# Two fused transformer blocks on one Trainium2 core: the second attention's rotation gets its swapped quarters by transfers inside SBUF in place of products with a swap matrix

## The reference, cut to what matters

```python
def rope_half(x, ang):
    n = x.shape[-1] // 2
    x1, x2 = x[..., :n], x[..., n:]
    cos, sin = jnp.cos(ang).astype(x.dtype), jnp.sin(ang).astype(x.dtype)
    return jnp.concatenate([x1 * cos - x2 * sin, x1 * sin + x2 * cos], axis=-1)

def axial_rope(x, row_ang, col_ang):
    return jnp.concatenate([rope_half(x[..., :AXIAL_DIM], row_ang),
                            rope_half(x[..., AXIAL_DIM:], col_ang)], axis=-1)
    ...
    q = axial_rope(rmsnorm_2(q.reshape(B, S, N_Q_HEADS, HEAD_DIM), q_gain), row_ang, col_ang)
    k = axial_rope(rmsnorm_2(k.reshape(B, S, N_KV_HEADS, HEAD_DIM), k_gain), row_ang, col_ang)
```

## Time and profile before

| | us |
|---|---|
| median of 3 runs (lowest, highest) | 1326.78 (1326.47, 1327.3) |
| the profiled execution | 1326.74 |
| its span from first to last instruction | 1325.0 |
| TensorE busy | 1264.7 (95%) |
| VectorE busy | 711.0 (54%) |
| ScalarE busy | 545.7 (41%) |
| GpSimd busy | 533.5 (40%) |

### The profile page before, as it was taken

How to read it: one execution, slowest core, us unless ns; L and a number is a source line. 1 busy time by engine, 2 the same in 40 slices (tenths; PEclk the granted TensorE clock), 3 DMA queues, 4 the chain that set the end, 5 groups by cost and what they waited for, 6 DMA issues and landing times.

```text
span 1325.0 us, 20731 instructions
## 1 busy us (share of the span) xinstructions
PE 1264.7 (95%) x8300; PEld 1003.5 (76%) x8300; DVE 711.0 (54%) x827; ACT 545.7 (41%) x734; POOL 533.5 (40%) x245
## 2 busy tenths in 40 slices
PE   5999999888899999999999999999999999999995
PEld 3777757677777877788888888888776777777873
DVE  8788756757559533336224143144477755442833
ACT  5332253244253433543223122235332468885342
POOL 4443222710157742274444444445443332223453
PEclk9999999989899999999999999999999999999998
DMA  6571111110045221122223332222422322112221
GB/s 218 160 229 64 64 48 53 59 35 4 12 158 163 100 78 51 48 96 96 95 95 96 101 102 100 96 96 96 144 88 80 108 75 65 64 65 67 99 90 64
DMA packets 35098, 119.91 MB, mean 91 GB/s; under 512 B 4544, under 2 KB 4672, under 8 KB 34624
## 3 DMA queue, kind: packets, MB, share of 16 engines
q1 hardware_dynamic: 29808, 105.78, 24.0%
q10 hardware_dynamic: 5200, 12.85, 3.1%
HBM read 111.01 MB, written 2.10 MB: 85 GB/s over the span
## 4 chain that ended last, share of the span: by engine, by line
PE 78%; DVE 14%; ACT 4%; issue 2%; ACTq 1%; DMA 1%; POOL 0%; DVEq 0%; SPq 0%
PE banks L1383 20%; PE banks L1385 19%; PE banks L1384 19%; DVE y_mid L831 2%; DVE tmp L831 1%; PE banks L1846 1%; PE banks L1404 1%; PE banks L1862 1%; PE banks L1406 1%; PE banks L1405 1%; PE banks L1951 1%; DVE qk L831 1%; PE banks L1936 1%; PE banks L1611 1%; DVE yk L831 1%
## 5 line engine op out<-in xcount | busy, mean ns | idle before, releaser
L338 POOL TENSOR_TENSOR w_lo<-w_raw,w_hi 128x1024 fp32r<-128x1024 f32 x145 | 353.7, 2440 | 536.9 <-ACT w_hi L401 536.7
L401 ACT ACTIVATE w_hi<-w_raw 128x1024 fp32r<-128x1024 f32 x145 | 153.9, 1062 | 333.2 <-PE banks L1385 213.1
L1383 PE MATMUL banks<-a_hi,w_hi 128*128 128x512 f32 x584 | 235.2, 403 | 15.5 <-DVE a_lo L839 13.4
L1385 PE MATMUL banks<-a_hi,w_lo 128*128 128x512 f32 x616 | 241.1, 391 | 0.0
L1384 PE MATMUL banks<-a_lo,w_hi 128*128 128x512 f32 x584 | 228.5, 391 | 0.0
L1385 PE MATMUL banks<-b_hi,w_lo 128*128 128x512 f32 x384 | 149.5, 389 | 0.0
L1383 PEld LDWEIGHTS banks<-a_hi,w_hi 128*128 128x128 f32 x584 | 110.1, 188 | 50.2 <-issue 17.8
L1385 PEld LDWEIGHTS banks<-a_hi,w_lo 128*128 128x128 f32 x616 | 116.2, 189 | 24.9
L831 DVE TENSOR_TENSOR x_res<-banks,x_res 128x512 f32<-128x512 f32 x56 | 38.7, 692 | 178.5 <-PE banks L1385 178.3
L338 POOL TENSOR_TENSOR w_lo<-w_raw,w_hi_mlp 128x1024 fp32r<-128x1024 f32 x36 | 87.3, 2425 | 107.7 <-ACT w_hi_mlp L401 107.7
L1384 PEld LDWEIGHTS banks<-a_lo,w_hi 128*128 128x128 f32 x584 | 110.3, 189 | 21.6 <-issue 0.7
(11 more groups left out here) (372 smaller groups left out, 2389.5 us busy)
## 6 DMA issues: line engine op xcount, KB each, us to landing
w_raw<-in_weights SPq DMA_DIRECT2D x189, 512.0 KB, 3.3
x_in<-in_x SPq DMA_DIRECT2D x4, 512.0 KB, 6.7
rot<-qk ACTq DMA_DIRECT2D x32, 64.0 KB, 2.1
decay<-in_decay ACTq DMA_DIRECT2D x1, 2048.0 KB, 8.9
x_res<-in_x ACTq DMA_DIRECT2D x4, 512.0 KB, 5.5
out_fm<-x_res SPq DMA_DIRECT2D x8, 256.0 KB, 2.1
consts<-in_consts SPq DMA_DIRECT2D x1, 1209.0 KB, 12.0
q_twice<-q_twice ACTq DMA_DIRECT2D x8, 128.0 KB, 3.6
```

The costliest lines, as they stand in the source:

```text
L338: nc.gpsimd.tensor_tensor(o, a, b, op).then_inc(S(name), 1)
L401: return nc.scalar.activation(o, a, f, **kw)
L1383: mm(o, high[:, w], hi[:, kc, :], start=kc == first, stop=False)
L1385: done = mm(o, w_lo[:, s % 4, w], hi[:, kc, :], start=False, stop=kc == last)
```

## The change

The swap matrix goes out of the constants and the product with it out of qk_norm. In its place ScalarE's queue gets swap_quarters(f): eight transfers of 16 partitions x 2 KB from qk2 to a new tile rot2 (two slots), in its iterations S_U (tiles 0 and 1), S_U+2, S_U+3 and S_GA (tiles 2, 3, 4). They stand behind head_hi and head_stack of the same iteration and ahead of gelu. They wait for the gains (qg_ready) and, from tile 2 on, until tile f-2 is rotated, whose slot they use. VectorE waits for their landing and reads rot2 where it read the bank. The minus sign of the swap matrix moves into the table of sines.

```diff
+        rot2 = at("rot2", 166, [P, 2, T])
...
+            def swap_quarters(f):
+
+                act.wait_ge(S("qg_ready"), f + 1)
+                if f >= 2:
+                    act.wait_ge(S("qk2_ready"), f - 1)
+                q = HD // 4
+                for r in range(0, P, q):
+                    o = r ^ q
+                    act.dma_start(rot2[o:o + q, f % 2, :], qk2[r:r + q, f, :]).then_inc(S(f"rot_loaded{f % 2}"), 16)
...
+                for f in {S_U: (0, 1), S_U + 2: (2,), S_U + 3: (3,), S_GA: (4,)}.get(s, ()):
+                    swap_quarters(f)
                 if S_U < s <= S_GA:
                     f = s - S_U - 1
                     act.wait_ge(S("tile_taken"), S_U + f + 1)
...
             def axial_rope(f):
 
-                dve.wait_ge(S("rot_done"), f + 1)
-                step(tt(tmp2[:, 0, :], psum[2 + f % 2][:], axial[:, 1, :], ALU.mult))
+                dve.wait_ge(S(f"rot_loaded{f % 2}"), 16 * (16 + 8 * (f // 2 + 1)))
+                step(tt(tmp2[:, 0, :], rot2[:, f % 2, :], axial[:, 1, :], ALU.mult))
...
                 if f >= 2:
                     pe.wait_ge(S("qk2_ready"), f - 1)
-                mm(psum[2 + f % 2][:], C("swap_ax"), qk2[:, f, :], start=True, stop=True).then_inc(S("rot_done"), 1)
                 spread_parts(psum[4 + f % 2][:], f, rn2_hi[0:10, :], rn2_lo[0:10, :]).then_inc(S("spread2_done"), 1)
...
-    axial = np.stack([np.cos(ang), np.sin(ang)], axis=1).astype(f32)
+    sign = np.where(i % half < quart, -1.0, 1.0)[:, None]
+    axial = np.stack([np.cos(ang), sign * np.sin(ang)], axis=1).astype(f32)
```

More of the change, by code:

```diff
@@ L55 @@
 CONSTS = [("eps6", 1), ("eps64", 1), ("inv_freq", 1), ("kg_scale", 1), ("kg_eps", 1), ("kg_min", 1),
-          ("ident", 128), ("ones", 128), ("blockones", 128), ("center", 128), ("swap_ax", 128),
+          ("ident", 128), ("ones", 128), ("blockones", 128), ("center", 128),
           ("cum_inc", 128), ("cum_exc", 128), ("mask_strict", CH), ("mask_inc", CH), ("mask_pair", CH),
@@ L2032, in shape_constants @@
     quart = HD // 4
-    t["swap_ax"] = (1.0 * ((row // half == col // half) & (col % half >= quart) & (row == col - quart))
-                    - 1.0 * ((row // half == col // half) & (col % half < quart) & (row == col + quart)))
     t["cum_inc"] = -EXP_HALF * (1.0 * (chunk & (row <= col)) - 1.0 * before_mid)
```

## The result

The changed kernel takes 1335.11 us (median of 6 runs, 1332.87 to 1338.18), the kernel before, run beside it, 1326.62 (6 runs, 1326.0 to 1329.16). The ratio is 1.0066, 95% interval 1.0055 to 1.0077: slower by 8.8 us, between 7.3 and 10.2. Forecast was 1332.4 in a range of 1326.5 to 1336.5. The profiled execution took 1332.87 us, its span 1331.1.

A forecast was written before the change was run, and what follows sets the result against it. TensorE was taken to bound the kernel; 40 issues on ScalarE's queue would make w_lo late, so despite 4.73 us less work TensorE ends slab S_GA+3 5.7 us later: 1326.74 + 5.7 = 1332.4 us, range 1326.5 to 1336.5.

The forecast's parts named there:

- the signs that were named: From 1010 to 1062 us: later splits, issue idle time, TensorE waiting for w_lo, chain on ScalarE's queue, first rotation step over 2 us.
- The price of an issue: On ScalarE's queue: 0.64 us per transfer behind a first of 0.51, so 5.0 us for eight, 10.1 for sixteen.
- The chain along ScalarE: From rn's square root to slab S_GA+3: 40 issues delay ScalarE's splits and w_lo, leaving TensorE 5.7 us later at the end.
- the blocked third step of tile 0: VectorE's rotation of tile 0: second w_lo blocks its third step to 1027.6, tile ready at 1028.4; without that stall 1025.6.
- the last slab: TensorE's slab S_GA+3, after a 4.6 us stall for w_lo: takes 5.44 us and a start of 0.1, ending at 1062.7.
- A smaller standstill: TensorE before slab S_GA+2: wanted w_lo at 1044.2, there at 1046.9, so 2.7 us stalled.
- VectorE's late tile: Tile of S_GA+2 taken at 1064.3 if w_lo blocks two VectorE steps, S_GB wanting it at 1062.7: +1.6, 1334.0; rival's chance 0.15.
- The rival of 1322.0: On ScalarE's queue the issues hide, so the whole saving of 4.73 us of TensorE products lands: 1322.0; chance 0.08.

The follow-up runs named there:

- SyncE's: The changed kernel with its 40 transfers unaltered but issued in SyncE's queue, behind the load of the slab four further on: 1324.72 us, ratio 0.9987 to the kernel before.
- sixteen-issue form: The changed kernel with 16 transfers instead of 40, eight of 16 partitions x 8 KB for tiles 0 to 3, eight for tile 4: 1322.24 us, ratio 0.9966.
- the execution with the filled standstill: The changed kernel with 20 unread products on TensorE behind slab S_GA+2, where it stood still for 4.86 us: 1333.94 us, ratio 1.0053 to the kernel before.

## Why the prediction was right, and where it was short

**The bound and the cause.** Right: TensorE without a gap before, ScalarE's queue on the chain after, and w_lo late. The removed products brought nothing, and the issue, not the landing, was the price (SyncE's and the sixteen-issue form show it). The runs divide the 8.9 us further: 5.9 go when swap 2 no longer waits for tile 0, which the forecast had as a wait on the same chain, and 3.0 are left with all 40 issues in place. (The 2.8 us of VectorE's held-up steps are a part of that wait and not a further term.) Of the signs that were named, one came only in part: the rotation's first VectorE step took over 2 us for tile 0 (2.44), and 0.69 for the other four. VectorE did wait for rot2, 2.65 and 2.86 us, but TensorE waited for w_lo and not for VectorE.

**The price of an issue.** Right to 1%: 16 in 10.18 us where 10.1 was reckoned, 8 in 5.00 where 5.0. The last eight took 5.34, one of them 0.92. The figure of a neighbour with twice the partitions carried over.

**The chain along ScalarE**, in us behind the square root's start:

| step | forecast | measured |
|---|---|---|
| split for S_U+3 | 10.27 | 10.31 |
| swap 2 starts | 18.77 | 18.76 |
| swap 3 starts | 27.8 | 27.86 |
| split for S_GA+2 | 33.7 | 33.72 |
| split for S_GA+3 | 43.9 | 44.34 |
| w_lo for S_GA+3 there | 47.5 | 47.82 |
| slab S_GA+3 ends | 53.0 | 56.13 |

Every step along ScalarE held, the blocked third step of tile 0 too. There two errors cancelled by luck: by the forecast's own rows the second w_lo runs from 1024.24 (0.08 us behind the w_hi that ends at 1024.16) to 1026.6, not from 1024.7 to 1027.1; it did start at that earlier place and took 2.71 us instead of 2.40. And the first w_lo held up the first step only because rot2 is read from SBUF. The kernel with both products and transfers has the bank as first source and is 2.8 us earlier there: the term belongs to the change, not to the stage.

**The term that was short: the last slab.** It was taken at 5.5 us, the length of a slab at full clock, and took 8.26. A standstill of TensorE was counted as its own length alone. The forecast had such a standstill (4.6 us, measured 4.86) and read the granted clock only for this stage of the kernel before, where it is 1.00 and TensorE never stands still. The same trace has a place that prices it: TensorE starts at 20.87 us behind a wait of 1.81, and from 20 to 25 us its clock has a mean of 0.70, with products 0.43 us apart. With these 2.8 us the sum is 1326.74 + 5.7 + 2.8 = 1335.2, against 1335.11. That the medians fit so well is in part chance, since the forecast is counted from one execution and the kernel's six runs spread over 5.3 us.

A smaller standstill fell out by the same cause: before S_GA+2 2.7 us were forecast and 1.12 measured, since slab S_GA+1 ran 3.5 us at half clock and ended that much later (clock 0.83 in the rows from 1034 to 1044). That cost nothing, for w_lo was later still.

**VectorE's late tile**, the term of 1.6 us left to a rival. The tile of S_GA+2 was taken at 1060.88, behind a step of head_lo of 2.76 us, as that rival had it; but the slow slab ended only at 1063.37, so nobody waited. At full clock it would have ended at 1060.6, and TensorE would have waited about 1 us (estimate): the term is there, covered by the one that the forecast lacked. Where ScalarE is not late, this is the wait of 1.71 us of the form with sixteen issues.

**The rival of 1322.0** was priced too well. It took the 4.73 us of products for the gain if nothing came against it. With no transfer at all the stage gains 1.91 us, with sixteen issues 2.25, because VectorE is next, with two late tiles of ga. For this rival the question "what is late next" was put to ScalarE alone; VectorE was 31.72 of 37 us busy in that stretch, and each slab became shorter for it. The medians show 3.7 and 4.5 us; the traced executions differ from the traced one before by 2.0 and 3.3, and where the rest lies is open.

## What to carry to other kernels

A transfer costs the queue that issues it: here about 0.61 us for 32, 64 or 128 KB alike. Count issues times their measured time, put them in the order of the engine, ask which of its other tasks stands behind them and which wait stands ahead of them: here 40 issues of 32 KB, one batch of them behind a wait for VectorE, cost 8.8 us, and 16 issues of the same bytes without that wait gained 4.5. Where TensorE will stand still, read what its clock does behind standstills of that length, for work at half clock is paid on top of the wait, unless another engine is later still. And when work is taken off the bound, ask every other engine, not only the one that is given work, for its time per slab against the new, shorter one.

## What the runs showed of the hardware that was not expected

- An issue between two tiles in SBUF took 611 ns on ScalarE's queue with 16 partitions of 2 KB, and eight took 4.94 us on SyncE's. The cost does not go with the queue, the partitions or the bytes: 16 partitions x 8 KB took 612 ns in the median. It goes in part with what was issued just before: SyncE's issue of a weight slab takes 0.33 us alone and took 0.58 right behind one of these, and the first of a batch took 0.51 in the changed kernel (1026.00). The landing did differ, 2.0 us in the median for 32 KB and 4.2 for 128 KB. The Trainium skill, "DMA: Bandwidth & Descriptors", section "Issuing engines are not separate DMA queues", calls the time to initiate usually small relative to the DMA; here it is 0.61 us against a landing of 2.0, and eight in a row hold the queue for 5.0 us.
- TensorE's clock fell to 0.50 behind a standstill of 4.86 us and stayed there for 5.5 us of work, and had a mean of 0.66 over the 5 us behind one of 3.10. It did not fall behind the first one of 1.57; behind that of 1.56 before S_GA+1 it did, 1.3 us after TensorE had started again (0.83 in the mean of 1034 to 1044), while in the execution with the filled standstill it did not behind the same wait of 1.53, but did behind the next of 2.69.
- Work that adds nothing to the result can make a kernel faster where it fills such waits: with the five products put back and the bank as VectorE's source the changed kernel was 4.6 us faster, 2.8 of them on ScalarE's chain by that source.
- VectorE's step with two sources in SBUF takes 0.69 us, and up to 2.8 where it meets one of GpSimd's w_lo of 2.4; with a bank as one source it takes 0.69 beside it (1022.48, w_lo from 1021.68 to 1024.04).
